# A hybrid encoder's mixer: the token indexer moved up behind its projection, the second state-space turn behind it, sums over heads as trees, attention on negated logits

## The reference

```python
for l in range(DEPTH):                                  # 2
    x = layer_norm(ALPHA * x + 0.5 * swiglu_ffn(x, ffn1_w_up[l], ffn1_w_down[l]), ...)
    x = layer_norm(ALPHA * x + hybrid_mixer(x, w_in[l], ...), ...)
    x = layer_norm(ALPHA * x + 0.5 * swiglu_ffn(x, ffn2_w_up[l], ffn2_w_down[l]), ...)

def hybrid_mixer(x, ...):
    u, q, k, v, qi, ki, wi, g_ssm, g_attn = split(x @ w_in)
    y_ssm  = ssm_branch(u, ...)       # states h_t = a*h_(t-1) + B u_t, complex; y = C h + d u; gelu; glu
    y_attn = dsa_branch(q, k, v, qi, ki, wi, rel_bias)
    return (sigmoid(g_ssm) * (y_ssm @ w_branch[0]) + sigmoid(g_attn) * (y_attn @ w_branch[1])) @ w_out

# dsa_branch, for each query (8 indexer heads of 32, 8 attention heads of 64)
score = sum_h wi[h] * relu(qi[h] . ki) * IDX_SCALE      # admissible keys only (chunks of 64)
sel   = top_k(score, 64)
p     = softmax(q . k[sel] * ATTN_SCALE + bias[t5_bucket(sel - pos)])
out   = p @ v[sel]
```

## Time and profile before

| | before |
|---|---|
| median of 3 runs | 1191.07 us (1190.71 to 1191.79) |
| the profiled execution: its own time | 1192.74 us |
| its span, first to last instruction | 1190.9 us |
| mean granted clock of TensorE | 0.986 |
| busy: TensorE / VectorE / ScalarE / GpSimd | 1149.2 / 776.8 / 554.4 / 410.8 us |
| mixer of layer 0, 207 to 400 us: TensorE busy | 181.2 of 193 us |
| mixer of layer 1, 794 to 990 us: TensorE busy | 184.5 of 196 us |

### The profile page before, as it was taken

The page is one execution under the profiler, slowest core; times in us unless marked ns, Lnnn a source line. Parts: engine busy times, 40 slices in busy tenths (PEclk is TensorE's granted clock), DMA queues, the critical chain, the costliest instruction groups (busy, mean ns, idle before and its releaser), DMA issues.

```text
span 1190.9 us, 17708 instructions
## 1 busy us (share of the span) xinstructions
PE 1149.2 (96%) x5932; PEld 933.9 (78%) x5932; DVE 776.8 (65%) x1108; ACT 554.4 (47%) x791; POOL 410.8 (34%) x567
## 2 busy tenths in 40 slices
PE   8999999997999999999999999999979999999997
PEld 6888788875777788887878888888757877888885
DVE  5657646778857875775486555478679667655544
ACT  5545443574455354443245444336635634545430
POOL 2889984107520178998700000020257001000001
PEclk9999999998999999999999999999989999999999
DMA  8766653642446476566457575535435365666640
GB/s 258 227 203 199 217 178 95 218 152 82 117 129 212 153 211 212 176 218 202 128 162 226 177 245 187 187 103 187 135 85 168 122 221 153 213 210 209 198 158 36
DMA packets 158720, 207.50 MB, mean 174 GB/s; under 512 B 13144, under 2 KB 107672, under 8 KB 158656
## 3 DMA queue, kind: packets, MB, share of 16 engines
q1 hardware_dynamic: 154928, 201.70, 53.4%
q10 hardware_dynamic: 2704, 3.36, 1.1%
q0 software_dynamic: 1024, 1.61, 0.8%
HBM read 205.56 MB, written 1.06 MB: 173 GB/s over the span
## 4 chain that ended last, share of the span: by engine, by line
PE 55%; POOL 18%; DVE 15%; issue 5%; ACT 5%; DMA 1%; SPq 0%; ACTq 0%; POOLq 0%; DVEq 0%
PE ps L705 17%; PE ps L707 17%; PE ps L706 16%; POOL small L1486 7%; DVE wlo L1135 7%; POOL b_bar L1486 3%; ACT whi L407 2%; POOL tab_c L1486 2%; POOL tab_s L1614 1%; POOL tab_s L1486 1%; DVE score L1306 1%; PE ps L732 1%; POOL tab_c L1611 1%; DMA raw<-in_ffn_w_up 1%; DVE gates L1280 1%
## 5 line engine op out<-in xcount | busy, mean ns | idle before, releaser
L1135 DVE TENSOR_TENSOR wlo<-raw,whi 128x1024 fp32r<-128x1024 f32 (+1 forms) x372 | 486.1, 1327 | 193.3 <-ACT whi L407 179.3
L407 ACT CAST whi<-raw 128x1024 fp32r<-128x1024 f32 (+1 forms) x372 | 386.2, 1046 | 291.9 <-PE ps L707 228.5
L705 PE MATMUL ps<-whi,xh 128*128 128x512 f32 (+1 forms) x1056 | 421.4, 399 | 9.0 <-DVE wlo L1135 9.0
L707 PE MATMUL ps<-whi,xl 128*128 128x512 f32 (+1 forms) x1056 | 411.6, 390 | 0.0
L706 PE MATMUL ps<-wlo,xh 128*128 128x512 f32 (+1 forms) x1056 | 410.4, 389 | 0.0
L705 PEld LDWEIGHTS ps<-whi,xh 128*128 128x128 f32 x1056 | 199.5, 189 | 55.7 <-DVE wlo L1135 15.6
L707 PEld LDWEIGHTS ps<-whi,xl 128*128 128x128 f32 x1056 | 199.2, 189 | 42.1
L706 PEld LDWEIGHTS ps<-wlo,xh 128*128 128x128 f32 x1056 | 199.7, 189 | 37.2
L1510 POOL TENSOR_TENSOR rstd<-var_eps,cst 128x1 f32<-128x1 f32 x12 | 18.2, 1519 | 549.7 <-DVE var_eps L1182 549.7
L705 PE MATMUL ps<-whi,hh 128*128 128x512 f32 x352 | 140.6, 400 | 0.0
L707 PE MATMUL ps<-whi,hl 128*128 128x512 f32 x352 | 138.3, 393 | 0.0
(11 more groups left out here) (192 smaller groups left out, 1130.5 us busy)
## 6 DMA issues: line engine op xcount, KB each, us to landing
raw<-in_ffn_w_up SPq DMA_DIRECT2D x352, 256.0 KB, 4.0
raw<-in_ffn_w_down SPq DMA_DIRECT2D x176, 256.0 KB, 3.1
raw<-in_w_in SPq DMA_DIRECT2D x128, 256.0 KB, 3.3
raw<-in_w_branch SPq DMA_DIRECT2D x32, 256.0 KB, 3.0
raw<-in_w_out SPq DMA_DIRECT2D x32, 256.0 KB, 4.4
bias_g<-bias_rows ACTq DMA_DIRECT2D x16, 192.0 KB, 3.3
raw<-in_w_in SPq DMA_DIRECT2D x16, 148.0 KB, 2.3
affine<-in_ln_g SPq DMA_DIRECT2D x4, 512.0 KB, 5.4
```

Of the source, the lines that this page charges most:

```text
L407: nc.scalar.copy(whi[:, s % RING, 0:w], raw[:, s % RAW, 0:w]).then_inc(S["hi_done"], 1)
L705: nc.tensor.matmul(o, ah, bh, start=start, stop=False)
L707: return nc.tensor.matmul(o, al, bh, start=False, stop=stop)
L1135: nc.vector.tensor_tensor(wlo[:, s % RING, 0:w], raw[:, s % RAW, 0:w], f32(whi[:, s % RING, 0:w]), ALU.subtract).then_inc(S["split_done"], 1)
```

## The change

- **Places on TensorE.** The two `ssm_in` go from behind (2,0,1) and (3,0,1) to behind (2,0,0) and (2,1,0); the indexer's transposes from (2,1,3) to (2,0,1); its three products from (3,1,0), (3,1,2), (4,0,1) to (2,1,2), (3,0,0), (3,1,0); the first `ssm_out` from (5,1,1) to (5,0,1).
- **ScalarE** copies all four quarters of `ssm_in`'s product to SBUF, and does the three `relu_read` earlier, with two `split_hi` between them instead of four.
- **VectorE** turns all quarters from SBUF in four instructions instead of six (two of them twice as wide, the temporary in `h_st`). Quarter 1 is turned and scanned behind the indexer's sums. `idx_add` is a tree of `tensor_tensor` instead of a `tensor_reduce`. `split_lo` of tiles s+16 to s+19 comes behind both `select`, not between them.
- **Attention** works on negated logits, so that the minimum is the negated maximum; line 1325 goes, the exponential gets scale -1.
- **Transition:** one `split_lo` inside `norm` of token half 0, two before `x_lo`, one behind it.
- **GpSimd** issues the first load of `c_raw` behind those of `b_raw`, before the tables instead of behind them.

```diff
-PAIR_IN = [(2, 0, 1), (3, 0, 1)]
-TURN_AT = [(1, 1, 1), (2, 1, 3), (3, 1, 3), (4, 0, 2)]
-IDX_AT = [(3, 1, 0), (3, 1, 2), (4, 0, 1)]
-OUT_AT = [(5, 1, 1), (6, 0, 1), (7, 0, 1), (7, 1, 3)]
+PAIR_IN = [(2, 0, 0), (2, 1, 0)]
+TURN_AT = [(1, 1, 1), (2, 0, 1), (3, 1, 3), (4, 0, 2)]
+IDX_AT = [(2, 1, 2), (3, 0, 0), (3, 1, 0)]
+OUT_AT = [(5, 0, 1), (6, 0, 1), (7, 0, 1), (7, 1, 3)]
 ATT_C = 6
...
     max8 = sb("max8", [P, 8])
-    row_max = sb("row_max", [P, COMBOS])
     neg_max = sb("neg_max", [P, COMBOS])
...
     stg = place("stg", [P, 2, NT, 512])
-    score_at = at[0]
-    g_tmp = place("g_tmp", [P, 4, HALF])
-    at[0] = score_at
     score = place("score", [P, NT, SEQ])
...
-            def bu_copy(l):
-                act.wait_ge(S["bu_done"], 2 * l + 2)
-                for q in (2, 3):
+            def bu_copy(l, half):
+                act.wait_ge(S["bu_done"], 2 * l + half + 1)
+                for q in (2 * half, 2 * half + 1):
                     at = (q % 2) * SEQ
...
                     part = prob[:, hd % 2, i * P:i * P + KEYS[i]]
-                    ins = nc.scalar.activation(part, part, ACT.Exp, bias=neg_max[:, a:a + 1],
+                    ins = nc.scalar.activation(part, part, ACT.Exp, bias=neg_max[:, a:a + 1], scale=-1.0,
                                                accum_out=row_sum[:, a:a + 1])
...
                 splits(s + 6, 2)
+                bu_copy(l, 0)
+                pt_read(l, 1)
                 proj_read(l, 2, 0)
-                splits(s + 8)
+                bu_copy(l, 1)
+                relu_read(l, 0)
+                splits(s + 8, 2)
                 proj_read(l, 2, 1)
-                pt_read(l, 1)
-                bu_copy(l)
+                relu_read(l, 1)
+                splits(s + 10, 2)
                 proj_read(l, 3, 0)
-                relu_read(l, 0)
+                relu_read(l, 2)
                 splits(s + 12)
...
                 pt_read(l, 2)
-                relu_read(l, 1)
-                relu_read(l, 2)
                 pt_read(l, 3)
...
             def transition(n, s, aff):
-                norm(n, s, 0, aff)
-                splits(s, 2)
+                norm(n, s, 0, aff, lambda: splits(s, 1))
+                splits(s + 1, 2)
                 x_lo(n + 1, 0)
-                splits(s + 2, 2)
+                splits(s + 3, 1)
                 norm(n, s, 1, aff, lambda: splits(s + 4, 1))
...
             def ssm_turn(l, q):
-                dve.wait_ge(S["bu_done"], 2 * l + q // 2 + 1)
-                co, si = quarter(tab_c, q), quarter(tab_s, q)
-                at = (q % 2) * SEQ
-                re, im = ps[:, BU:BU + 4, at:at + HALF], ps[:, BU:BU + 4, at + HALF:at + 2 * HALF]
-                g = turned_in(q)
-                g_re, g_im, t = g[:, 0], g[:, 1], g_tmp[:, :, :]
-                nc.vector.tensor_tensor(g_re, re, co, ALU.mult)
-                link(nc.vector.tensor_tensor(t, im, si, ALU.mult))
-                link(nc.vector.tensor_tensor(g_re, g_re, t, ALU.add))
-                nc.vector.tensor_tensor(g_im, im, co, ALU.mult)
-                nc.vector.tensor_tensor(t, re, si, ALU.mult).then_inc(S["bu_read"], 1)
                 dve.wait_ge(S["bu_read"], NQ * l + q + 1)
-                link(nc.vector.tensor_tensor(g_im, g_im, t, ALU.subtract))
-            def ssm_turn_sb(l, q):
-                dve.wait_ge(S["bu_read"], NQ * l + q + 1)
-                co, si = quarter(tab_c, q), quarter(tab_s, q)
-                g = turned_in(q)
-                g_re, g_im, t1, t2 = g[:, 0], g[:, 1], g_tmp[:, :, :], g_tmp2[:, :, :]
-                nc.vector.tensor_tensor(t1, g_im, si, ALU.mult)
-                link(nc.vector.tensor_tensor(t2, g_re, si, ALU.mult))
-                nc.vector.tensor_tensor(g_re, g_re, co, ALU.mult)
-                link(nc.vector.tensor_tensor(g_im, g_im, co, ALU.mult))
-                nc.vector.tensor_tensor(g_re, g_re, t1, ALU.add)
-                link(nc.vector.tensor_tensor(g_im, g_im, t2, ALU.subtract))
+                if q >= 2:
+                    dve.wait_ge(S["y_used"], NQ * l + q - 1)
+                co = quarter(tab_c, q).unsqueeze(1).to_broadcast([P, 2, 4, HALF])
+                si = quarter(tab_s, q).unsqueeze(1).to_broadcast([P, 2, 4, HALF])
+                g, t = turned_in(q), h_st[:, q % 2, :, :, 1:]
+                link(nc.vector.tensor_tensor(t, g[:, ::-1], si, ALU.mult))
+                link(nc.vector.tensor_tensor(g, g, co, ALU.mult))
+                nc.vector.tensor_tensor(g[:, 0], g[:, 0], t[:, 0], ALU.add)
+                link(nc.vector.tensor_tensor(g[:, 1], g[:, 1], t[:, 1], ALU.subtract))
             def ssm_scan(l, q):
...
             def idx_add(l, n):
...
                 dve.wait_ge(S["weighted"], len(IDX_BATCH) * l + n + 1)
-                if n == 0:
-                    out, src = score[:, 0, 0:P], relu[:, 0:4, :].rearrange("p b (u n) -> p n (b u)", n=P)
-                elif n == 1:
-                    out, src = relu[:, 4, :], relu[:, 0:4, :].rearrange("p b n -> p n b")
+                link(nc.vector.tensor_tensor(relu[:, 0:2, :], relu[:, 0:2, :], relu[:, 2:4, :], ALU.add))
+                if n == 1:
+                    out, a, b = relu[:, 4, :], relu[:, 0, :], relu[:, 1, :]
                 else:
-                    dve.wait_ge(S["idx_added"], len(IDX_BATCH) * l + n)
-                    out, src = score[:, 1, :], relu[:, :, :].rearrange("p b n -> p n b")
-                nc.vector.tensor_reduce(out, src, mybir.AxisListType.X, ALU.add).then_inc(S["idx_added"], 1)
+                    link(nc.vector.tensor_tensor(relu[:, 0, :], relu[:, 0, :], relu[:, 1, :], ALU.add))
+                    if n == 0:
+                        out, a, b = score[:, 0, 0:P], relu[:, 0, 0:P], relu[:, 0, P:2 * P]
+                    else:
+                        out, a, b = score[:, 1, :], relu[:, 0, :], relu[:, 4, :]
+                nc.vector.tensor_tensor(out, a, b, ALU.add).then_inc(S["idx_added"], 1)
             def select(l, i):
...
                     a, cols = NT * hd + i, slice(i * P, i * P + KEYS[i])
+                    dve.wait_ge(S["dve_chain"], chain[0])
                     hold()
                     end = (2 + i) * P
-                    link(nc.vector.tensor_tensor_reduce(
+                    ins = nc.vector.tensor_tensor_reduce(
                         out=prob[:, hd % 2, cols], in0=ps[:, score_bank(hd), cols],
-                        in1=bias_g[:, hd % 2, end - KEYS[i]:end][:, ::-1], scale=1.0, scalar=-3.0e38, op0=ALU.add,
-                        op1=ALU.max, accum_out=row_max[:, a:a + 1]))
-                a = NT * hd
-                nc.vector.tensor_scalar(neg_max[:, a:a + 2], row_max[:, a:a + 2], -1.0, None, ALU.mult
-                                        ).then_inc(S["neg_max_ready"], 1)
+                        in1=bias_g[:, hd % 2, end - KEYS[i]:end][:, ::-1], scale=-1.0, scalar=3.0e38, op0=ALU.add,
+                        op1=ALU.min, accum_out=neg_max[:, a:a + 1])
+                ins.then_inc(S["neg_max_ready"], 1)
             def invert(l, hd):
...
                 ssm_turn(l, 0)
+                ssm_scan(l, 0)
+                idx_add(l, 0)
+                splits(s + 8, 2)
+                idx_add(l, 1)
+                splits(s + 10, 2)
+                idx_add(l, 2)
+                splits(s + 12, 2)
                 ssm_turn(l, 1)
-                ssm_scan(l, 0)
-                splits(s + 8)
                 ssm_scan(l, 1)
-                idx_add(l, 0)
-                splits(s + 12)
-                idx_add(l, 1)
-                idx_add(l, 2)
+                splits(s + 14, 2)
                 select(l, 0)
+                select(l, 1)
                 splits(s + 16)
-                select(l, 1)
                 def gate_merge(t):
...
                     if j == 1:
-                        ssm_turn_sb(l, 2)
+                        ssm_turn(l, 2)
                     if j == 3:
...
                     if j == 7:
-                        ssm_turn_sb(l, 3)
+                        ssm_turn(l, 3)
                     if j == 9:
...
             def m(n):
...
+            def load_c(l, q):
+                for v, name in enumerate(("ssm_c_re", "ssm_c_im")):
+                    src = A[name].rearrange("l (q g) n s -> l q (g n) s", q=NQ)[l, q]
+                    pool.dma_start(c_raw[:, v, :, :], src.unsqueeze(1).to_broadcast([P, 2, STATE])
+                                   ).then_inc(S["c_landed"], 16)
             def prepare(l):
...
                                            ).then_inc(S["b_landed"], 16)
+                hold()
+                load_c(l, 0)
                 pool.wait_ge(S["sincos_ready"], l + 1)
...
                         pool.wait_ge(S["bt_done"], NQ * l + q)
-                    hold()
-                    for v, name in enumerate(("ssm_c_re", "ssm_c_im")):
-                        src = A[name].rearrange("l (q g) n s -> l q (g n) s", q=NQ)[l, q]
```

(8 more changed lines are left out.)

## The result

| | before | after |
|---|---|---|
| median of 20 runs each | 1191.16 us (1189.53 to 1193.27) | 1193.16 us (1190.52 to 1195.47) |
| ratio, with its 95% interval | | 1.0016 [1.0009, 1.0023] |
| the profiled execution: its own time, its span | 1192.74, 1190.9 us | 1190.59, 1188.6 us |
| mean granted clock of TensorE | 0.986 | 0.988 |

The change costs 1.9 us (1.1 to 2.7), where 1190.8, and so no change, had been forecast. A second profile of the same kernel (the first experiment) is needed to see why.

A forecast was written before the change was run, and what follows sets the result against it. TensorE, busy for 96% of the span, bounds the kernel, so only standing or half-clock time can go. +9.6 - 5.2 - 4.7 = -0.3 us takes the span from 1190.9 to 1190.6; median forecast 1190.8, range 1176 to 1198.

The forecast's parts named there:

- The `ssm_in` stall: TensorE at the first `ssm_in` in its new place: a new stall of 1.3 us, waiting for the indexer's `proj_read`.
- The contention: VectorE between third sum and mask: eight instructions each pay 1.05 us beside GpSimd's rotation, 8.4 us in all.
- The mask: VectorE's second mask in layer 0: ready at 293.3 us, with bounds of 284.9 and 295.4.
- The transition: Five TensorE waits behind transitions, before FFNs and mixers, go: 4.7 us gained, bounds 2 and 5.5.
- The stall at head 6: TensorE's 0.94 us wait at head 6's transposes and the half-clock stretch behind it go: 2.6 us per layer.
- a loss of 4.8 us per layer, 9.6 in all: Head 0's transposes in the attention come at 306.1 instead of 301.34 us, because mask and queued loads are late.
- 4.3 later: Between mask and attention: from the last split's end at 297.9 to the tile being taken at 302.2, 4.3 us.
- The late gain: Attention at head 6, by line 1325 going: 2.6 us per layer, 5.2 in all; 0 if VectorE is late again.
- GpSimd doesn't get in the way: Rival: no contention, mask at 284.9, 8.4 us per layer better, 1174.0; chance 0.18, half-way (1182.4) 0.10.
- The late stall stays: Rival, slower: the wait at head 6's transposes stays, 2.6 us per layer, 1196.0; chance 0.16.
- Nothing moves: Rival: mask as late as before and the rest small; counted inside the forecast, with no chance of its own.
- a new half-clock stretch: Rival: half clock behind the 1.3 us stall at `ssm_in` moves the chain 1.7 us per layer, 1194.2; chance 0.09.

The follow-up runs named there:

- the first experiment: The kernel after, without any edit, profiled a second time: 1191.58 us, ratio 1.0011 to the kernel before; its profiled execution took 1193.85 us.
- the held rotation: The kernel after with GpSimd's first rotation held until quarter 1 is scanned: 1183.78 us, ratio 0.9945 to the kernel before.
- the order alone: The kernel after with the new transition, negated logits and early load of `c_raw` taken back: 1202.38 us, ratio 1.0100 to the kernel before.
- The experiment with the exponentials first: The kernel after with ScalarE's four `split_hi` of s+20 to s+23 moved behind the first two heads' exponentials: 1188.89 us, ratio 0.9975 to before.
- the three side edits alone: The kernel before with the new transition, negated logits and early load of `c_raw`, mixer's order unchanged: 1179.19 us, ratio 0.9900.
- the small ones with one piece of the large: The kernel before with new transition, negated logits, early load of `c_raw`, and `idx_add` as a tree: 1175.28 us, ratio 0.9871.
- the last version: The kernel after with rotation held, exponentials first, first `ssm_out` back behind (5,1,1), one split between the selections: 1175.81 us, ratio 0.9870 to before.

## Why the prediction was right or wrong

**Right, with sizes.** The `ssm_in` stall: 0.65 us in the first trace and 1.34 in the second, 1.3 forecast. The third sum: ends at 257.2, forecast 259.2 less the 1.4 of the earlier start, 257.8. The contention: 18.9 us forecast from the third sum to the first selection, 18.6 measured, and the held rotation shows its cause. It was worth 7.9 us (6.8 between the rows of after and of the held rotation, and the 1.1 by which the last two splits are long in both), not 8.4: the scans paid 1.7 us, which the sum left out, and each pair of splits 1.1 instead of 2.1. The Trainium skill ("SBUF — State Buffer", section "SBUF: two separate sides") says that instructions of VectorE with two SBUF inputs share a locked port pair with GpSimd; by that the scans pay too, and the trace agrees: 4.01 us beside 2.34. The mask: 290.3, forecast 291.9 on this clock. The two new waits in front of (5,1) and (6,0), and the queue of loads behind them: right in place. The transition: 4.35 us by the marks and 4.4 by the ratio, 4.7 forecast. The stall at head 6 and its half clock: gone, in every trace of this kernel. Here the reason was half luck: the negation alone removes them on the kernel before, as forecast, but the new order alone removes them too, and the prediction gave the whole to line 1325 going.

**The step that failed** is the term "a loss of 4.8 us per layer, 9.6 in all", in the part from the mask to the attention. The mechanism was right and the size wrong: measured, down to head 1's transposes, are 6.6 us per layer. The term was counted to head 0's transposes, and TensorE's own arrival there was put at "302.8 to 306.1", with "up to 3.3 more at half" clock under cover of the late exponential. The first trace is that upper case: half clock until 300.7, 0.41 and 0.24 us of wait, 4.8 and 4.2 us of loss at head 1. In the other six layers TensorE is there 1.7 to 4.3 us before the exponential, and a further stretch at 1.2 GHz stands behind that wait, 1.4 to 2.8 us more between head 0 and head 1. The loss at head 1 in the eight layers of the four traces with this order (the first, the second, that with the old load of `c_raw`, that of the order alone) is 4.8, 4.2, 7.5, 6.2, 8.0, 8.2, 7.7 and 6.0 us, 6.6 on average (the 8.2 with the half-clock stretch at `ssm_in` in it). These executions took 2.6 us less, 2.3 more, 3.1 more and 0.5 less than the median of the runs each was made with, so the average leans a little to the slow side. At head 0, where the forecast stopped counting, it is 5.2 on average; the other 1.4 is the stretch behind the wait. The 5.2 instead of 4.8 hide two sizes: the step "4.3 later", from the last split to the tile being taken, measured 5.3 to 6.8 us in these layers, 5.8 on average, and the mask came 0.8 to 1.6 us sooner than forecast in seven of the eight.

Such a stretch was among the rivals, at `ssm_in`; there the clock stayed full in seven of the eight layers (1.00 from 230 to 240 us in the second trace) and fell in one, behind the wait of 1.85 us shown above. The forecast didn't look for it at the wait that it made itself, the one at head 0. The experiment with the exponentials first shows that the late exponential is the cause: without that wait there is no such stretch, and 4.9 us come back.

**The late gain** was put at 2.6 us per layer. From head 1's transposes to the end of the mixer the three traces of after and of after with the old load give back 2.9 to 4.1, 3.5 on average. The order alone gives back 1.8 of that. So the net of the two is 2.9 us per layer by the traces, where 2.2 was forecast.

**A term of nothing that wasn't nothing.** "(c) The load of `c_raw` moves within one queue between the same two ends: nothing." The ends were the same, the work between them not: the issue sat right in front of the instructions for which TensorE waits. It gives 3.0 us by the traces, 3.2 (1.4 to 5.0) by the medians.

**The sum, redone.** By the marks, on average over the three traces with all the parts of the mixer's change, the two mixers add 5.9 us (2.6, 5.7 and 9.4) against 9.6 - 5.2 = 4.4 in the forecast. The transitions give 4.35 and the load 3.0, and the slower products of the FFNs, which no step of the prediction knew, cost 3.1. That makes 5.9 - 4.35 - 3.0 + 3.1 = 1.65, and 1.9 (1.1 to 2.7) was measured. In words: the forecast's -0.3 becomes +1.65 by 1.5 more in the mixers, 0.35 less from the transitions, 3.1 from the products and 3.0 back from the load. The last two were both outside the forecast and all but cancel, so that the total came out near is in that part luck.

**The rivals.** "GpSimd doesn't get in the way" fell with the 18.6 us; but even with the contention held off the gain over after was 8.5 us and not the forecast's 16.8, for the first exponential stays late. "The late stall stays" fell. "Nothing moves" fell by a little, and "a new half-clock stretch" was right in kind and, but for one layer in eight, wrong in place.

**What stays open.** Why TensorE's clock comes back at 295 in one execution and at 300.7 in another of the same kernel, no run here tells. How the late gain divides between the negation and TensorE's lateness is settled only roughly: the negation gives 4.5 us alone on the kernel before; within the new order the traces leave it 1.7 us per layer, 3.4 in two, and the medians 0.0100 - 0.0037 - 0.0027 - 0.0016 = 0.0020, 2.4 us with an uncertainty as large. And which part of the program makes the FFNs' products follow each other more slowly is open; the order alone and the three side edits alone don't.

## What to carry to other kernels

When work is moved ahead on one engine, price every queue behind the wait that results: here a load that waits for a split of VectorE held four ScalarE instructions, these the first exponential, and that wait cost a second time in clock. A wait that "TensorE's half clock will cover" should be priced for both cases, since the same kernel shows both. And a change of many parts that moves nothing should be taken apart before it is kept or dropped: here 12 us of gain in three small edits lay under 12 us of loss in the large one, and the small ones with one piece of the large are as fast as the best of the new order.

## What the runs showed of the hardware

- Two executions of one kernel can differ by the stretches at half clock alone: 10.4 us at 0.51 in front of head 0 in one, 3.3 in front of it and 3.2 behind it in another. A single pair of traces had the wrong sign here (-2.2 us, where the medians say +1.9).
- Scans are lengthened beside GpSimd nearly as much as additions of the same size: two took 4.01 us instead of 2.34 (0.8 each), an addition 1.68 instead of 0.69.
- A wait of TensorE of 0.65 to 1.34 us at `ssm_in`, among full passes, left the clock at 1.00, as did waits of 1.48 and 1.69 in the last version; one of 1.85 had 3.4 us at 0.50 behind it. One of 1.7 to 4.3 at head 0 was followed by 1.2 GHz in all six layers in which it occurred in the four traces with this order.
- Issuing a pair of transfers on GpSimd's queue takes it 1.5 us. With it moved in front of a long chain of GpSimd's, that chain was 2.3 us shorter, not longer, in the traces of before and after.
- TensorE's products can follow each other at two rates at the same full clock and without waits: 229 ns apart on average in the first FFN of the kernel before and 232.5 in that of the kernel after, in every trace of either, which makes 3.1 us over the whole program.
